# The recurrent mixer's second half as one pipeline

## Chip, cores and metric

The kernel runs on 1 core of one Trainium2 chip. The metric is the device time of one execution in microseconds.

## The reference

Two blocks of a language model run on one sequence of 256 tokens, width 1024, in float32. The second block's first mixer is the part that matters here. It projects the tokens to r, k, v and low-rank parts, and to a convolution branch. The recurrent half runs, for each of 8 heads of 64,

```python
s_kk = jnp.einsum('bhvk,bhk->bhv', state, kk_t)
state = (state * w_t[:, :, None, :] - s_kk[..., None] * (kk_t * a_t)[:, :, None, :]
         + v_t[..., None] * k_t[:, :, None, :])
y_t = jnp.einsum('bhvk,bhk->bhv', state, r_t)
```

then normalises y by head, adds a bonus `sum(r k r_k) v` and gates it. The other half is a causal convolution of 31 taps by channel (512 channels), a layer norm and a SiLU. Both halves, concatenated, go through a 1024 x 1024 output projection, an RMS norm and the next feed-forward.

## The kernel before

The five engines each run one program written by hand; semaphores order them. Weights come as units of 128 x 2048 floats by SP's queue into `wf[s]`; ScalarE copies each to a rounded high part `wh[s]` (`prep`, L614), VectorE subtracts to the low part `wl[s]` (`low`, L1070), and TensorE forms each product as three matmuls (L1790 to L1792).

The recurrence is computed in two chunks b of 128 tokens, by heads in four groups g = 2b + parity, four heads each. Rows (alpha, beta, rho, kappa) are turned to `rows_T` (L2142). Gram products of rows give, for each group, a strictly lower matrix N. Its inverse is built by merging blocks: from pairs (D and its transpose DT), in six rounds m, with Z = mask(N D), then D from DT Z, and DT from Z DT. A round has for each group four matmuls for Z ("z_mm"), a mask by VectorE (L1517, from a bank), four for D and four for DT (L2200), and copies to SBUF by ScalarE (L902). All four Z products of a round stand ahead of its D and DT products.

Before the rounds come the other Gram products: key Grams (L2179) and beta Grams (L2159), which VectorE takes from the banks with a mask (L1521 and L1517). In the rounds VectorE runs the convolution's taps (L1536) on three of the four channel tiles; the fourth tile's taps are made by ScalarE (a scaled copy, L917) and added by GpSimd (L569). GpSimd also forms products for the bonus and the gate (L547, L557, L563) and the first DT (L553). `v` is mixed with its shifted self on VectorE (L1446, L1450, L1456).

Behind the rounds: key times value (`first_w`, L2226), the solve (`solved`, L2233), the state between the chunks (L2254, L2255), the outputs (`outputs_of`, L2242, L2243), the turns of the convolution (L2262), its norm (L1611 to L1624), the head norm of y in `centred`, `spread` and `gated_y`, and the output projection (`second_exit`): block 0 is turned whole (L1837), four units are multiplied for it and, with block 1 turned in the middle, `half` is signalled. ScalarE's order at the exit is: both `take_x` (L619), `prep(4)`, `prep(5)`, the squares of block 0 (L641). The next feed-forward's loads are issued when both chunks' outputs are done.

## Time and profile before

| | |
|---|---|
| median of 3 runs | 2488.04 us (2486.35 to 2489.47) |
| profiled execution | 2487.75 us |
| its span | 2485.9 us |
| mean granted TensorE clock | 0.985 |
| TensorE, VectorE, ScalarE, GpSimd busy | 97, 59, 43, 6% |
| the stretch of the change | about 1570 to 1750 us |

PE is TensorE's matmuls, PEld its weight loads, DVE VectorE, ACT ScalarE, POOL GpSimd. A row of a timeline has its start in us, its length, engine, line, operation, tiles, shapes and count; in brackets the idle time before it and what ended it. A float32 matmul has two entries, a transpose one. `arena`, `wf`, `gains`, `y` and `hid` are memories that many names of the kernel share: `wf` holds N, D, DT and Z here. Names in the rows are those of the memory.

### The profile page before, as it was taken

Reading aid. Unit: us, or ns where it says so; the run is one execution under the profiler, and the core shown is the slowest. Engines: PE = TensorE matmul, PEld = TensorE weight load, DVE = VectorE, ACT = ScalarE, POOL = GpSimd, SP = SyncE. Lnnn points to the kernel's source line nnn. Section 1 sums busy time; section 2 is a strip of 40 time slices with the busy share of each in tenths; the row PEclk is TensorE's granted clock in tenths of the full one; section 3 lists DMA queues with packets and bytes.
Section 4 is the critical chain, followed back from the end, with each engine's and each line's share of the span. In section 5 each row is a group of like instructions: output and inputs, shape, how many; then the busy total and the mean of one; then the engine's idle time right before and its main releaser. Section 6 shows DMA issues by size and latency. Waiting matters only on the chain.

```text
span 2485.9 us, 29666 instructions
## 1 busy us (share of the span) xinstructions
PE 2399.5 (97%) x11556; PEld 1982.3 (80%) x11556; DVE 1458.1 (59%) x1569; ACT 1080.6 (43%) x1335; POOL 150.5 (6%) x178
## 2 busy tenths in 40 slices
PE   6999998999999999999999999898999999999998
PEld 5888887888888888778887887697888888777887
DVE  3545766754645667675456456984545545645544
ACT  4434445343443444544444445353444444545442
POOL 0001000000000000000000002431000000200000
PEclk9999999999999999999999999998999999999999
DMA  6666444555655564455565565203556556343552
GB/s 218 206 207 214 171 136 150 203 171 186 204 180 186 199 205 170 136 187 179 186 218 170 190 226 175 72 1 133 178 191 199 179 191 200 115 139 119 191 190 92
DMA packets 281236, 426.57 MB, mean 172 GB/s; under 512 B 11747, under 2 KB 193635, under 8 KB 281136
## 3 DMA queue, kind: packets, MB, share of 16 engines
q1 hardware_dynamic: 272768, 399.67, 48.6%
q0 software_dynamic: 7520, 25.37, 3.3%
q8 instruction: 58, 0.95, 0.2%
q10 hardware_dynamic: 864, 0.36, 0.1%
q14 instruction: 26, 0.21, 0.0%
HBM read 422.49 MB, written 1.05 MB: 170 GB/s over the span
## 4 chain that ended last, share of the span: by engine, by line
PE 82%; DVE 12%; ACT 2%; issue 2%; POOL 2%; DMA 1%; SPq 1%; DVEq 0%; POOLq 0%; ACTq 0%
PE bank L1790 24%; PE bank L1792 24%; PE bank L1791 24%; DVE wl L1070 4%; PE bank L2200 2%; PE bank L1890 1%; PE bank L1837 1%; POOL rstd L445 1%; DVE stats L1105 1%; DVE arena L1536 1%; SPq L341 1%; DVE x L1114 1%; DVE y L1172 1%; PE bank L1992 1%; DVE y L1139 1%
## 5 line engine op out<-in xcount | busy, mean ns | idle before, releaser
L1070 DVE TENSOR_TENSOR wl<-wf,wh 128x2048 fp32r<-128x2048 f32 x355 | 809.4, 2293 | 416.2 <-ACT wh L614 415.8
L1790 PE MATMUL bank<-wh,xTh 128*128 128x512 f32 x2336 | 931.5, 399 | 34.9 <-DVE xTl L1084 26.9
L1792 PE MATMUL bank<-wh,xTl 128*128 128x512 f32 x2336 | 914.4, 391 | 0.0
L1791 PE MATMUL bank<-wl,xTh 128*128 128x512 f32 x2336 | 913.6, 391 | 0.0
L614 ACT ACTIVATE wh<-wf 128x2048 fp32r<-128x2048 f32 x355 | 673.4, 1915 | 248.9 <-PE bank L1792 244.4
L1790 PEld LDWEIGHTS bank<-wh,xTh 128*128 128x128 f32 x2336 | 442.8, 190 | 128.6 <-DVE xTl L1084 29.6
L1792 PEld LDWEIGHTS bank<-wh,xTl 128*128 128x128 f32 x2336 | 442.0, 189 | 94.2
L1791 PEld LDWEIGHTS bank<-wl,xTh 128*128 128x128 f32 x2336 | 443.1, 190 | 87.6 <-issue 0.7
L1790 PE MATMUL bank<-wh,hTh 128*128 128x512 f32 x704 | 276.9, 393 | 0.1
L1792 PE MATMUL bank<-wh,hTl 128*128 128x512 f32 x704 | 274.5, 390 | 0.0
L1791 PE MATMUL bank<-wl,hTh 128*128 128x512 f32 x704 | 274.0, 389 | 0.0
L623 ACT ACTIVATE sil<-bank 128x256 f32<-128x256 f32 x176 | 60.4, 381 | 298.9 <-PE bank L1792 298.9
L1792 PEld LDWEIGHTS bank<-wh,hTl 128*128 128x128 f32 x704 | 132.1, 188 | 27.8
L1790 PEld LDWEIGHTS bank<-wh,hTh 128*128 128x128 f32 x704 | 132.2, 188 | 26.9 <-DVE wl L1070 0.3
L1791 PEld LDWEIGHTS bank<-wl,hTh 128*128 128x128 f32 x704 | 132.3, 188 | 26.5
L1089 DVE SCALAR_TENSOR_TENSOR hid<-sil,bank 128x256 f32<-128x256 f32 x176 | 68.2, 418 | 132.2 <-ACT sil L623 131.7
L445 POOL TENSOR_TENSOR rstd<-ve,mhalf 128x1 f32<-128x1 f32 x42 | 36.8, 877 | 1730.4 <-DVE ve L1109 857.8
L679 ACT ACTIVATE hTh<-bank 128x512 fp32r<-128x512 f32 x64 | 38.3, 598 | 218.7 <-PE bank L1890 218.7
L1217 DVE TENSOR_TENSOR hTl<-bank,hTh 128x512 fp32r<-128x512 f32 x64 | 44.3, 692 | 110.3 <-ACT hTh L679 110.3
L619 ACT ACTIVATE xTh<-bank 128x512 fp32r<-128x512 f32 x76 | 41.3, 596 | 104.8 <-PE bank L1837 104.4
L2200 PE MATMUL bank<-wf 128*128 128x128 f32 x544 | 64.9, 283 | 7.7 <-DVE wf L1517 7.7
L2200 PEld LDWEIGHTS bank<-wf 128*128 128x128 f32 x544 | 63.8, 198 | 8.8 <-DVE wf L1517 8.2
(317 smaller groups left out, 1554.8 us busy)
## 6 DMA issues: line engine op xcount, KB each, us to landing
wf<-in_ffn_w SPq DMA_DIRECT2D x160, 512.0 KB, 4.8
wf<-in_w_in SPq DMA_DIRECT2D x52, 1024.0 KB, 5.4
wf<-in_ffn_w SPq DMA_DIRECT2D x44, 1024.0 KB, 5.2
wf<-in_ffn_w_down SPq DMA_DIRECT2D x44, 1024.0 KB, 5.1
wf<-in_ffn_w_gate SPq DMA_DIRECT2D x80, 512.0 KB, 4.0
wf<-in_ffn_w_up SPq DMA_DIRECT2D x80, 512.0 KB, 4.9
wf<-in_w_branch SPq DMA_DIRECT2D x16, 1024.0 KB, 5.2
wf<-in_c_w_in SPq DMA_DIRECT2D x14, 1024.0 KB, 5.9
```

Source lines behind the costliest of these rows:

```text
L445: pool.tensor_tensor(dst, src, mhalf[:, 0:n], ALU.pow).then_inc(SEM[to], 1)
L614: act.activation(wh[s], wf[s], ACT.Copy).then_inc(SEM[f"hi{s}"], 1)
L619: act.activation(xTh[:, 4 * r:4 * r + 4, b * P:(b + 1) * P], bank[banks[r]][:, :].rearrange("p (k t) -> p k t", k=4), ACT.Copy).then_inc(S ...
L623: act.activation(sil[:, b, :], bank[bk][:, 0:STEP], ACT.Silu).then_inc(SEM["h_silu"], 1)
L679: act.activation(hTh[0][:, :, :], bank[6][:, :].rearrange("p (k t) -> p k t", k=2), ACT.Copy)\
L1070: dve.tensor_tensor(wl[s], wf[s], wh[s].bitcast(f32), ALU.subtract).then_inc(SEM[f"lo{s}"], 1)
L1089: return dve.scalar_tensor_tensor(hid[:, b, :], sil[:, b, :], half, bank[bk][:, STEP:2 * STEP], ALU.mult, ALU.mult)
L1217: dve.tensor_tensor(hTl[0][:, :, :], bank[6][:, :].rearrange("p (k t) -> p k t", k=2), hTh[0][:, :, :].bitcast(f32), ALU.subtract).then_in ...
L1790: pe.matmul(o, lh, rh, start=start, stop=False)
L1791: pe.matmul(o, lh, rl, start=False, stop=False)
L1792: return pe.matmul(o, ll, rh, start=False, stop=stop)
L2200: ins = pe.matmul(bank[bk][:, i * P:(i + 1) * P], left[:, i, :], right[:, i, :], start=True, stop=True)
```

## The change

The Gram products other than those of N leave their place ahead of the merges. The merges run as 24 steps i (group i % 4, round i // 4 + 1): at step i TensorE forms Z of i, then D and DT of i - 2, and from step 5 to 16 one of the twelve Gram products (`FILLS`). ScalarE copies a Gram product to SBUF and GpSimd masks it there. Taps of all four channel tiles run on VectorE, one a step, two in the odd steps from 9 on. The v mixing stands behind the first masks; its last addition is GpSimd's. The row turns of four groups are split around the last v unit. Key-times-value products and the state's kappa part stand between merges. At the exit the projection is split by its input half: convolution half first, then y's half, and each half block is turned, copied and lowered by itself. SP loads two units of the next feed-forward when the last merge product is done, two more after the outputs.

```diff
-    gram_bank = (1, 3, 0, 2)
+    start_bank, z_bank, fill_bank = (1, 3, 4, 5), (1, 3), (0, 2)
+    FILLS = [("key", u) for u in range(4)] + [("beta", g) for g in range(2)] + [("key", u) for u in range(4, 8)] + [("beta", g) for g in (2, 3)]
+    FIRST_FILL = 3
...
-        for h in range(2):
-            half_panel(w_ab, HALF, 2 + h, h)
+        half_panel(w_ab, HALF, 2, 1)
+        half_panel(w_ab, HALF, 3, 0)
         half_panel(w_ab, 0, 1, 1)
+        sp.wait_ge(SEM["dt_mm"], c.next("dt_mm", 24))
+        up(w1[0, 1], w3[0, 1], 1, 0)
         sp.wait_ge(SEM["y_mm"], c.next("y_mm", TB))
-        ffn(w1[0, 1], w3[0, 1], w2[0, 1])
+        up(w1[0, 1], w3[0, 1], 0, 4)
+        ffn(w1[0, 1], w3[0, 1], w2[0, 1], led=True, next_led=True)
...
         shift(kp, kq, "prev0_ld")
-        shift(kp, kq, "prev1_ld")
 
...
             pool.wait_ge(SEM["n_ready"], c.next("n_ready"))
-            pool.tensor_tensor(DT_t[g], N_t[g], four(pair_t), ALU.mult).then_inc(SEM["dt_ready"], 1)
+            pool.tensor_tensor(DT_t[g], N_t[g], four(pair_t), ALU.mult).then_inc(SEM["dt0_ready"], 1)
+        shift(kp, kq, "prev1_ld")
+        pool.wait_ge(SEM["v_out"], c.next("v_out"))
+        pool.wait_ge(SEM["prev1_ld"], c.next("prev1_ld", 64))
+        pool.tensor_tensor(rv_t, rv_t, kp, ALU.add).then_inc(SEM["v_in"], 1)
         pool.wait_ge(SEM["late_ld"], c.next("late_ld", 16 * 6))
-        pool.wait_ge(SEM["rk_ready"], c.next("rk_ready"))
-        product(r_t, r_t, k_new)
-        pool.tensor_tensor(r_t, r_t, both(r_k), ALU.mult).then_inc(SEM["rk_made"], 1)
-        pool.wait_ge(SEM["bonus_done"], c.next("bonus_done"))
-        for b in range(TB):
-            product(heads(r_t[:, b, :]), heads(rv_t[:, b, :]), per_head(bonus[:, 8 * b:8 * b + 8]))
-        product(r_t, r_t, both(lnx_b), ALU.add)
-        product(r_t, r_t, g_t)
-        pool.tensor_tensor(g_t, g_t, both(lnx_g), ALU.mult).then_inc(SEM["post_made"], 1)
-        pool.wait_ge(SEM["tap0"], c.next("tap0"))
-        for n in range(CONV - 1):
-            pool.wait_ge(SEM["tap_in"], c.next("tap_in"))
-            if n:
-                pool.wait_ge(SEM["tap"], c.next("tap"))
-            pool.tensor_tensor(conv_o[:, 3, :], conv_o[:, 3, :], tap_s[:, n % 4, :], ALU.add).then_inc(SEM["tap"], 1)
-        c.count("tap")
+        for f, (kind, n) in enumerate(FILLS):
+            pool.wait_ge(SEM["gram_cp"], c.next("gram_cp"))
+            if kind == "key":
+                t = k_grams[n // 2][:, 2 * (n % 2):2 * (n % 2) + 2, :, :]
+                m = gram_m.rearrange("p (a w) t -> p a w t", a=1).broadcast_to([P, 2, 2, P])
+            else:
+                t, m = b_grams[n], four(gram_m[:, 1, :])
+            pool.tensor_tensor(t, t, m, ALU.mult).then_inc(SEM["gram_made"], 1)
+            if f == 0:
+                pool.wait_ge(SEM["rk_ready"], c.next("rk_ready"))
+                product(r_t, r_t, k_new)
+            elif f == 1:
+                pool.tensor_tensor(r_t, r_t, both(r_k), ALU.mult).then_inc(SEM["rk_made"], 1)
+            elif f in (7, 8):
+                if f == 7:
+                    pool.wait_ge(SEM["bonus_done"], c.next("bonus_done"))
+                b = f - 7
+                product(heads(r_t[:, b, :]), heads(rv_t[:, b, :]), per_head(bonus[:, 8 * b:8 * b + 8]))
+            elif f == 9:
+                product(r_t, r_t, both(lnx_b), ALU.add)
+            elif f == 10:
+                product(r_t, r_t, g_t)
+            elif f == 11:
+                pool.tensor_tensor(g_t, g_t, both(lnx_g), ALU.mult).then_inc(SEM["post_made"], 1)
...
-        for g in range(4):
-            take_rows(g, ROW_A)
+        for g in (0, 2):
+            take_rows(g, ROW_A, 4 + g)
+        prep(3)
+        for g in (1, 3):
+            take_rows(g, ROW_A, 4 + g)
+        for g in range(2):
+            take_rows(g, ROW_R, 6 + g)
         prep(1)
-        for g in range(4):
-            take_rows(g, ROW_R)
-
...
-        n = 0
-        for m in range(1, 7):
-            for g in range(4):
-                if m < 6:
-                    copied(D_t, g, 4, "d_mm", "d_ready")
-                copied(DT_t, g, 6, "dt_mm", "dt_ready")
-                for _ in range(2 if g == 3 else 1):
-                    tap(n)
-                    n += 1
-        act.wait_ge(SEM["tap"], c.next("tap", CONV - 1))
-        taken(w_s, 0, 4, "w_mm", "w_ready")
-        taken(u_s, 0, 5, "u_mm", "u_ready")
-        taken(w_s, 1, 1, "w_mm", "w_ready")
-        taken(u_s, 1, 3, "u_mm", "u_ready")
+        for g in range(2, 4):
+            take_rows(g, ROW_R, 4 + g)
+        c.count("gram_mm", 4)
+        for i in range(24):
+            if i < 20:
+                copied(D_t, i, 4, "d_mm", "d_ready")
+            copied(DT_t, i, 6, "dt_mm", "dt_ready")
+            if i == FIRST_FILL:
+                act.wait_ge(SEM["v_in"], c.next("v_in"))
+            if 0 <= i - FIRST_FILL < len(FILLS):
+                take_gram(i - FIRST_FILL)
+            if i == 17:
+                taken(w_s, 0, 0, "w_mm", "w_ready")
+        act.wait_ge(SEM["rk_made"], c.next("rk_made"))
+        taken(u_s, 0, 4, "u_mm", "u_ready")
+        taken(w_s, 1, 2, "w_mm", "w_ready")
...
-        y_squares(0)
+        def out_x(b, r, bk):
+            act.wait_ge(SEM["tr"], c.next("tr"))
+            act.activation(xTh[:, 4 * r:4 * r + 4, b * P:(b + 1) * P], bank[bk][:, :].rearrange("p (k t) -> p k t", k=4), ACT.Copy)\
+               .then_inc(SEM["xt_hi"], 1)
+
         for b in range(TB):
             silu_conv(b)
+        taken(u_s, 1, 4, "u_mm", "u_ready")
+        y_squares(0)
+        out_x(0, 1, 6)
+        out_x(1, 1, 7)
         y_squares(1)
+        out_x(0, 0, 4)
+        out_x(1, 0, 5)
         c.count("gen1", 3)
         c.count("gen0", 3)
-        for b in range(TB):
-            take_x(b)
         prep(4, 2)
         prep(5, 2)
         out_of_mixer(RMS)
...
-        c.count("gen0")
-        unmixed(rv_t, mu_v, 0, 1)
...
         def tap(j):
-            if j == 0:
-                dve.tensor_scalar(conv_o[:, 3, :], gluT[:, 3, 0:T], convw[:, 3, 0:1], convw[:, 3, CONV:CONV + 1], ALU.mult, ALU.add)\
-                   .then_inc(SEM["tap0"], 1)
-            for ct in range(3):
-                dve.wait_ge(SEM["dve"], c.so_far("dve") - 2)
+            for ct in range(4):
+                dve.wait_ge(SEM["dve"], c.so_far("dve") - 3)
...
-        mixed_in(rv_t, kp, "prev1_ld").then_inc(SEM["v_in"], 1)
+        c.count("gen0")
+        unmixed(rv_t, mu_v, 0, 1)
+        dve.sem_inc(SEM["v_out"], 1)
         for g in range(4):
-            masked(D_t[g], gram_bank[g], pair_m, "turned", "d_ready")
-        dve.wait_ge(SEM["v_in"], c.next("v_in"))
+            masked(D_t[g], start_bank[g], pair_m, "turned", "d0_ready")
+        low(1)
         dve.wait_ge(SEM["cw_ready"], c.next("cw_ready"))
-        for u in range(4):
-            key_grams(u)
-        low(1)
-        for u in range(4, 8):
-            key_grams(u)
-        tap(0)
-        for g in range(4):
-            masked(b_grams[g], 4 + g, gram_m[:, 1, :], "gram_mm", "gram_ready")
-        dve.wait_ge(SEM["rk_made"], c.next("rk_made"))
-        dve.tensor_reduce(bonus, r_t.rearrange("p b (h n) -> p (b h) n", n=HD), X, ALU.add).then_inc(SEM["bonus_done"], 1)
         dve.wait_ge(SEM["lo1"], c.so_far("lo1"))
-        j = 1
-        for m in range(1, 7):
-            for g in range(4):
-                masked(Z_t[g], gram_bank[g], merge_m[m], "z_mm", "zp_ready")
-                for _ in range(2 if g % 2 and m < 5 else 1):
-                    if j < CONV:
-                        tap(j)
-                        j += 1
-        while j < CONV:
-            tap(j)
-            j += 1
+        j = 0
+        for i in range(24):
+            masked(Z_t[i % 4], z_bank[i % 2], merge_m[i // 4 + 1], "z_mm", "zp_ready")
+            if i == 8:
+                dve.wait_ge(SEM["rk_made"], c.next("rk_made"))
+                dve.tensor_reduce(bonus, r_t.rearrange("p b (h n) -> p (b h) n", n=HD), X, ALU.add).then_inc(SEM["bonus_done"], 1)
+            for _ in range(2 if i % 2 and i > 8 else 1):
+                if j < CONV:
+                    tap(j)
+                    j += 1
+        assert j == CONV
         dve.wait_ge(SEM["dve"], c.so_far("dve"))
         dve.sem_inc(SEM["conv_done"], 1)
...
-        dve.wait_ge(SEM["post_made"], c.next("post_made"))
-        centred(0)
...
+        centred(0)
+        out_x(0, 1, 6)
+        out_x(1, 1, 7)
         spread(0)
+        centred(1)
+        dve.wait_ge(SEM["post_made"], c.next("post_made"))
         gated_y(0)
-        centred(1)
         spread(1)
+        out_x(0, 0, 4)
         gated_y(1)
-        for b in range(TB):
-            take_x(b)
+        out_x(1, 0, 5)
         low(4)
         low(5)
...
         whole_unit(3, 0, outs(0))
-        whole_unit(1, 1, outs(0))
...
-        for g in range(4):
-            turn_rows(g, (alpha, beta))
+        for g in (0, 2):
+            turn_rows(g, (alpha, beta), 4 + g)
+        whole_unit(1, 1, outs(0))
+        for g in (1, 3):
+            turn_rows(g, (alpha, beta), 4 + g)
...
-        for g in range(4):
-            turn_rows(g, (rho, kappa))
-        pe.wait_ge(SEM["rows_ready"], c.next("rows_ready", 4))
-
...
+        for g in range(2, 4):
+            pe.wait_ge(SEM["rows_ready"], c.next("rows_ready"))
+            turn_rows(g, (rho, kappa), 4 + g)
+
+        def fill(f):
+            kind, n = FILLS[f]
+            if f == 0:
+                pe.wait_ge(SEM["gen0"], c.so_far("gen0"))
+            if f > 1:
+                pe.wait_ge(SEM["gram_cp"], c.next("gram_cp"))
+            o = bank[fill_bank[f % 2]]
+            if kind == "key":
+                b, par = n // 4, n // 2 % 2
+                for i in range(2):
+                    ins = pe.matmul(o[:, i * 2 * P:(i + 1) * 2 * P], row(b, par + 4 * (n % 2) + 2 * i, ROW_K),
+                                    rows_T[b][par * HD:(par + 1) * HD, 2 * (n % 2) + i, ROW_A:ROW_R + 1, :], start=True, stop=True)
+            else:
+                for q in range(4):
+                    h = 2 * q + n % 2
+                    ins = pe.matmul(o[:, q * P:(q + 1) * P], row(n // 2, h, ROW_B), row(n // 2, h, ROW_R), start=True, stop=True)
+            ins.then_inc(SEM["gram_mm"], 1)
...
-        pe.wait_ge(SEM["dt_ready"], c.next("dt_ready", 4))
-        for m in range(1, 7):
-            for g in range(4):
-                pe.wait_ge(SEM["d_ready"], c.next("d_ready"))
-                four_products(gram_bank[g], N_t[g], D_t[g], "z_mm")
-            if m == 1:
-                pe.wait_ge(SEM["gram_ready"], c.next("gram_ready", 4))
-            for g in range(4):
-                pe.wait_ge(SEM["zp_ready"], c.next("zp_ready"))
-                pe.wait_ge(SEM["dt_ready"], c.so_far("dt_ready") + max(0, g - 1))
-                if m < 6:
-                    pe.wait_ge(SEM["d_ready"], c.so_far("d_ready") + max(0, g - 1))
-                    four_products(4 + g % 2, DT_t[g], Z_t[g], "d_mm")
-                four_products(6 + g % 2, Z_t[g], DT_t[g], "dt_mm")
-            c.count("dt_ready", 4)
-
...
+        def z_products(i):
+            if i < 4:
+                pe.wait_ge(SEM["d0_ready"], c.next("d0_ready"))
+            else:
+                pe.wait_ge(SEM["d_ready"], c.so_far("d_ready") + i - 3)
+            if i > 1:
+                pe.wait_ge(SEM["zp_ready"], c.so_far("zp_ready") + i - 1)
+            four_products(z_bank[i % 2], N_t[i % 4], D_t[i % 4], "z_mm")
+
+        def merge_products(i):
+            g = i % 4
+            pe.wait_ge(SEM["zp_ready"], c.so_far("zp_ready") + i + 1)
+            if i < 4:
+                pe.wait_ge(SEM["dt0_ready"], c.next("dt0_ready"))
+            if i > 1:
+                pe.wait_ge(SEM["dt_ready"], c.so_far("dt_ready") + i - 1)
+            if i < 20:
+                if i > 1:
+                    pe.wait_ge(SEM["d_ready"], c.so_far("d_ready") + i - 1)
+                four_products(4 + g % 2, DT_t[g], Z_t[g], "d_mm")
+            four_products(6 + g % 2, Z_t[g], DT_t[g], "dt_mm")
...
+        for i in range(24):
+            z_products(i)
+            if i == 2:
+                pe.wait_ge(SEM["rows_ready"], c.next("rows_ready", 2))
+            if i > 1:
+                merge_products(i - 2)
+            if 0 <= i - 2 - FIRST_FILL < len(FILLS):
+                fill(i - 2 - FIRST_FILL)
+            if i == 18:
+                pe.wait_ge(SEM["gram_cp"], c.next("gram_cp", 2))
+                pe.wait_ge(SEM["gram_made"], c.next("gram_made", len(FILLS)))
+                pe.wait_ge(SEM["v_in"], c.next("v_in"))
+                key_values(0, 0, 0, True, True).then_inc(SEM["w_mm"], 1)
+            if i == 20:
+                key_values(1, 2, 0, True, False)
+            if i == 22:
+                pe.wait_ge(SEM["w_ready"], c.so_far("w_ready") + 1)
+                key_values(0, 0, 1, True, False)
+        pe.wait_ge(SEM["d_ready"], c.next("d_ready", 20))
+        state_of(kappa, rv_t, True, False)
+        merge_products(22)
+        pe.wait_ge(SEM["dt_ready"], c.so_far("dt_ready") + 22)
+        solved(0, 4)
+        merge_products(23)
         pe.wait_ge(SEM["u_ready"], c.next("u_ready"))
-        for h in range(RH):
-            o = bank[4][(h % 2) * HD:(h % 2 + 1) * HD, (h // 2) * HD:(h // 2 + 1) * HD]
-            pe.matmul(o, tokens(kappa, 0, h), tokens(rv_t, 0, h), start=True, stop=False)
-            ins = pe.matmul(o, tokens(beta, 0, h), tokens(u_s, 0, h), start=False, stop=True)
-        ins.then_inc(SEM["s_mm"], 1)
-        outputs_of(0, 0)
+        state_of(beta, u_s, False, True).then_inc(SEM["s_mm"], 1)
+        updates_out(0, 0)
+        pe.wait_ge(SEM["zp_ready"], c.next("zp_ready", 24))
+        key_values(1, 3, 1, True, False)
+        pe.wait_ge(SEM["state_in"], c.next("state_in"))
+        state_in(2, ROW_A, True).then_inc(SEM["w_mm"], 1)
+        state_in(3, ROW_R, False)
+        pe.wait_ge(SEM["dt_ready"], c.next("dt_ready", 24))
         pe.wait_ge(SEM["conv_done"], c.next("conv_done"))
-        pe.wait_ge(SEM["tap"], c.next("tap", CONV - 1))
...
+        for b in range(TB):
+            pe.wait_ge(SEM["yb_ready"], c.next("yb_ready"))
+            turn_half(y_conv[:, b, :], 6 + b)
+        pe.wait_ge(SEM["ya_ready"], c.next("ya_ready"))
+        turn_half(y_rwkv[:, 0, :], 4)
+        x_in()
+        part_unit(1, 1, 0, 0, True, False)
+        part_unit(2, 1, 0, 1, True, False)
+        x_in()
+        x_in()
+        part_unit(0, 0, 0, 0, False, True)
+        part_unit(3, 0, 0, 1, False, True).then_inc(SEM["half"], 1)
+        part_unit(1, 1, 1, 2, True, False)
+        pe.wait_ge(SEM["yc_ready"], c.next("yc_ready", TB))
+        pe.wait_ge(SEM["ya_ready"], c.next("ya_ready"))
+        turn_half(y_rwkv[:, 1, :], 5)
+        part_unit(2, 1, 1, 3, True, False)
+        x_in()
+        part_unit(0, 0, 1, 2, False, True)
+        turn(0, y, "x_ready")
+        part_unit(3, 0, 1, 3, False, True)
+
```

## Rows read from the trace of the kernel before

**Rows 1.** The page, part 1: busy time and share of the span

```profile
PE 2399.5 (97%) x11556; PEld 1982.3 (80%) x11556; DVE 1458.1 (59%) x1569; ACT 1080.6 (43%) x1335; POOL 150.5 (6%) x178
```

**Rows 2.** The chain that ended last, 1560 to 1760: start, us, what

```profile
1609.07 6.89 DVE arena L1536 x6
```

**Rows 3.** Windows: busy us and count by engine, granted clock, DMA share, GB/s

```profile
1603.00:1616.00 13.00, 6.40 (x55) 6.02 (x54) 13.00 (x13) 3.18 (x6) 10.96 (x7) 1.00 0.00 1
1616.60:1673.50 56.90, 56.42 (x483) 55.91 (x483) 50.25 (x104) 32.68 (x65) 19.30 (x25) 0.97 0.00 1
1673.50:1711.00 37.50, 25.84 (x192) 24.83 (x191) 15.73 (x30) 8.33 (x15) 7.57 (x9) 0.74 0.22 68
```

**Rows 4.** Timeline of VectorE: start, us, line, operation, count, idle before

```profile
1579.67 1.29 DVE L1517 TENSOR_TENSOR wf<-bank,gains 128x512 f32<-128x512 f32 x2
...
1585.60 2.29 DVE L1456 TENSOR_TENSOR arena<-arena 128x1024 f32<-128x1024 f32 x1
...
1603.30 0.68 DVE L1517 TENSOR_TENSOR wf<-bank,gains 128x512 f32<-128x512 f32 x1
...
1605.89 2.57 DVE L1536 SCALAR_TENSOR_TENSOR arena<-y,arena 128x256 f32<-128x256 f32 x1
1608.39 0.68 DVE L1517 TENSOR_TENSOR wf<-bank,gains 128x512 f32<-128x512 f32 x1
1608.99 4.45 DVE L1536 SCALAR_TENSOR_TENSOR arena<-y,arena 128x256 f32<-128x256 f32 x2
...
1618.26 2.45 DVE L1536 SCALAR_TENSOR_TENSOR arena<-y,arena 128x256 f32<-128x256 f32 x6
...
1671.96 0.64 DVE L1581 MEMSET y<- 64x256 f32 x2
```

**Rows 5.** Timeline of GpSimd, 1581 to 1622

```profile
1581.71 2.81 POOL L553 TENSOR_TENSOR wf<-wf,gains 128x512 f32<-128x512 f32 x2 [2.09 <-DVE wf L1543]
...
1603.46 2.23 POOL L547 TENSOR_TENSOR arena<-arena,gains 128x512 f32<-128x512 f32 x2 [9.72 <-DVE gains L1565]
1605.77 2.41 POOL L547 TENSOR_TENSOR arena<-arena,sil 128x1024 f32<-128x1024 f32 x1
...
1621.26 0.72 POOL L569 TENSOR_TENSOR arena<-arena 128x256 f32<-128x256 f32 x1 [6.38 <-ACT arena L917]
```

**Rows 6.** Timeline of TensorE, 1576 to 1675

```profile
1576.11 1.91 PE L2142 MATMUL bank<-ident,arena 128*128 128x128 f32 x16
1577.97 1.16 PE L2159 MATMUL bank<-rows_T 64*128 64x128 f32 x16
...
1586.32 2.96 PE L2179 MATMUL bank<-rows_T 64*128 64x256 f32 x16
...
1616.61 54.34 PE L2200 MATMUL bank<-wf 128*128 128x128 f32 x464 [5.44 <-DVE wf L1517]
...
1673.30 1.90 PE L2226 MATMUL bank<-arena 128*128 128x64 f32 x16
```

**Rows 7.** Timelines of all engines in the tail and the exit, 1691 to 1735

```profile
1691.27 0.70 DVE L1611 BATCH_NORM_STATS2 stats<-bank 128x6 f32<-128x512 f32 x1
...
1695.09 1.42 DVE L1624 SCALAR_TENSOR_TENSOR arena<-arena,rstd 128x512 f32<-128x512 f32 x2
...
1711.01 0.76 PE L1790 MATMUL bank<-wh,xTh 128*128 128x512 f32 x1 [7.11 <-DVE xTl L1084]
...
1720.17 3.72 ACT L614 ACTIVATE wh<-arena 128x2048 fp32r<-128x2048 f32 x2
1722.12 4.50 DVE L1070 TENSOR_TENSOR wl<-arena,wh 128x2048 fp32r<-128x2048 f32 x2 [1.00 <-ACT wh L614]
1725.10 0.60 ACT L641 ACTIVATE y<-bank 128x512 f32<-128x512 f32 x1 [1.20 <-PE bank L1792]
1727.88 1.92 ACT L614 ACTIVATE wh<-wf 128x2048 fp32r<-128x2048 f32 x1 [1.51 <-PE bank L1792]
1733.69 1.09 PE L1837 MATMUL bank<-ident,y 128*128 128x128 f32 x8 [0.47 <-DVE y L1128]
```

173 lines of the change are left out of this document (75 added, 98 removed).

## The prediction

> **What bounds the kernel now.** I read the page first: TensorE is busy 97% of the span [rows 1]. The change touches only the recurrent mixer's second half, about 1570 to 1750 us, so I read that stretch by windows [rows 3], where three kinds of time show. From 1603 to 1616 VectorE is busy all 13.0 us and TensorE 6.4. From 1616.6 to 1673.5 TensorE is busy 56.4 of 56.9. From 1673.5 to 1711 nobody is full and the granted clock averages 0.74. The chain of work that ended last says the same: it runs through VectorE taps up to 1616 (6.89 us for six of them [rows 2]) and then through merge products that follow each other without a wait [rows 6].
>
> **One VectorE tap and one GpSimd instruction.** Six taps in a row take 2.45 us [rows 4]; with 0.47 us for the last that is a pitch of 0.396. The tap that starts at 1605.89, just behind a GpSimd product of 2.41 us, takes 2.57 [rows 4, 5]. A mask that reads a bank starts inside the next GpSimd product, takes its usual 0.68 and hands over 0.60 later, at 1608.99 [rows 4]. So a tap, with both its tiles in SBUF, waits for GpSimd, and a mask does not. The rate comes from 1603.90 to 1615.88: 11.98 us hold nine taps (3.56) and one mask (0.60), so 7.8 us are waiting, while GpSimd was busy about 10.5 us (10.96 in the window less 0.44 before [rows 3, 5]). That is 0.74 us of VectorE per microsecond of GpSimd.
>
> The Trainium skill ("SBUF — State Buffer", the section on the two separate sides) has a rule that speaks against this change: VectorE with two SBUF inputs and GpSimd take turns on one port pair as an exclusive lock, and the loser waits for the whole instruction. By that rule the price would be 1.0 per microsecond, and the sum below some 8 us longer; the row's 2.57 beside 2.41 agrees with it, and the average 0.74 only says how often something else fills the wait.
>
> **The front, to the first merge mask.** The first Gram mask is at 1579.67 now [rows 4]. The change puts two groups of row turns (0.5 each, four take 1.91) ahead of the last v unit, which ends 1576.1 now; one group and a Gram set (1.2) follow [rows 6]: last turn 1577.5, copy 0.6, Gram set 1578.3 to 1579.5. The mask starts where it did. Masks and identities go on to 1585.6 as now [rows 4]. Then the v mixing (2.6), four masks (2.4) and the unit's low part (2.29) come: first merge mask at 1593.0, against 1603.30 [rows 4]. A gain of 10.3 us at this point, all of it from Gram masks and a bonus reduction moved behind it.
>
> **The pipeline on TensorE.** 58 products in 54.34 us are 0.937 each [rows 6]. From the first mask's end 66 of the 68 remain: 61.8. Filling: a key pair of half-array matmuls takes 0.75 to 0.86 (four pairs in 2.96 [rows 6] where pairs of both halves overlap; alone 4 x 0.216), a beta set 0.9; twelve come to 10.6. Three sets of key times value at 1.9 [rows 6], the kappa part 0.9 and the first solve 1.9 now stand before the last merge: 8.5. Sum 80.9, end 1674.6 if nothing waits. The merges end now just before the key times value set at 1673.30 [rows 6]. So on TensorE alone the pipeline gives nothing but later work done early (about 10 us of it).
>
> **The pipeline on VectorE.** 24 masks at 0.60 are 14.4; 31 taps of four instructions, 124 at 0.396, are 49.1 (34 more instructions than now); the reduction 1.2. Sum 64.7. The Gram masks are no longer there, and the taps that GpSimd and ScalarE did are. On GpSimd: v addition 2.4; twelve Gram products at 1.26 (a masked 128x512 product is between 1.04 and 1.40, [rows 5]), 15.1; two 128x1024 products 4.8, two halves 2.2, three more 7.2. Sum 31.7, all beside taps; today 30 additions of 0.73 lie there and 14 us of products, part of these beside bank masks. At 0.74 VectorE waits 23.5. Together 88.2: VectorE ends its taps at **1681**, against 1671.96 now, where the state's memset starts [rows 4]. Bounds: rate 0 leaves TensorE's 1674.6 as the limit (taps end near 1672); rate 1.0 gives 1689. I take 0.74, because the products at 1603 to 1615 are the same instructions beside the same taps. A check by parts: steps 0 to 8 have slack on VectorE (2.18 a step against 3.7 on TensorE) and hide some waits; steps 9 to 17 have none: 27.6 clean plus 0.74 x 21 of GpSimd is 43, against 34 on TensorE. In these steps TensorE waits for masks.
>
> **The tail to the first exit unit.** Around the last mask TensorE still owes the products of sets 21 to 23, kappa part and first solve (6.5), a copy (0.8), then beta part, outputs, key times value, state products and conv transposes (7.4): transposes end about 1692.7. The conv normalisation takes 5.2 (1691.27 to 1696.51, [rows 7]). ScalarE has the copy of the second solve queued behind both SiLUs: it lands near 1699, though the solve ended near 1695. Outputs 1.8, turns 0.9, copy and two low parts 1.9; VectorE's second centring is queued behind these low parts. Spread, centring and gating are six instructions 512 wide at 0.7 and two small ones (4.6 with their waits for each other), the turn 0.5: 1708.7. About 2 us more for the lower clock, which this tail has now too (0.74), gives 1710.7. The first exit unit is at 1711.01 now, after a wait of 7.11 [rows 7]. So the overlap of conv half and y half is real, and the 9 us late pipeline eats it.
>
> **The exit.** Four units from the first to the end of `half` take 13.9 now with a turn in between (1711.01 to 1725.0), without it 13.1: 1723.8. ScalarE squares at once today (1725.10), because both copies of the next feed-forward's units were done while TensorE worked (1720.17, 3.72) [rows 7]. After the change the turn of y's second block stands behind part unit (1,1,1), and ScalarE's order is turn copy, two unit copies, squares: 1723.8 + 2.7 + 0.5 + 0.8 + 3.7 = 1731.5. VectorE's second low part ends at 1733.9, against 1726.6 now [rows 7]. From there to the turn of the new x is 7.1 as now [rows 7]: **1741.0 against 1733.69**, +7.3. TensorE ran out of work near 1733 and waits 8 us; behind the 7.11 us wait at 1711 now, ten matmuls have a pitch of 0.43 (the first takes 0.76, [rows 7]) where the later ones have 0.23, and the same again costs 2.0.
>
> **Units loaded early** I cost at nothing. The copy at 1727.88 waits for TensorE (1.51), not for a load, and those at 1720.17 wait for the turn [rows 7]. If that cover were gone, a late load could cost at most what the copies that wait for it take, 3.7 us; an earlier one gives back nothing.
>
> **Sum.** +7.3 + 2.0 = +9.3 on the profiled execution's 2487.75 (span 2485.9 and 1.85 around it; median of the runs 2488.04, so no correction): **2497 us**. Within 0.2% (5 us) counts as no change.
>
> **Rivals.**
> 1. *TensorE bounds the pipeline*; GpSimd's instructions fall where VectorE waits anyway. For it: slack of 1.5 us in each early step. Against: from step 9 every second step has eight tap instructions. Taps end 1672, first exit unit 1702, turn of x 1732.5, with the clock's 2 us: 2488.5, no change. It ends on the faster side, at 2482, where TensorE in the tail then keeps the upper clock of 2.4 GHz (this tail's clock of 0.74 [rows 3] loses about 6). It decides where VectorE's exposed waiting is under 15 us instead of 23.5 (rate 0.47); above 19 us the time leaves the 5 us that count as no change.
> 2. *The clock falls inside the pipeline.* Today 5.4 us of waiting before 1616.61 is followed by a stretch at the lower of the two levels (1.2 GHz); in steps 13 to 16 TensorE has about 4 us of work in 10. Each 3 products there cost 2.3 more: +5 to +8, 2502 to 2505.
> 3. *The loads or the v shift are late.* The v addition waits for a transfer issued behind four GpSimd products; if the first Gram copy waits for it, +3: 2500.
>
> **Chances.** Forecast 0.54; rival 1 0.28 (half of it below 2483); rival 2 0.12; rival 3 0.06. The likeliest case's own range, from GpSimd products at 1.04 or 1.40 and the rate 0.6 to 0.85, is 2492.5 to 2502. For 8 in 10: 2487 to 2504. Faster takes rival 1's lower half (0.15); the same its upper half and the lowest tenth of the other cases (0.23); slower is the rest, 0.62.
>
> **What would show it.** First mask of the merges near 1593; VectorE full from there to about 1681 with tap instructions well above 0.47 wherever GpSimd runs; TensorE waiting for VectorE masks in the middle third; a wait of ScalarE for the last turn, and squares near 1731; TensorE idle for about 8 us before the turn of x. I am wrong if taps keep 0.47 beside GpSimd products, if TensorE's products run in one piece, or if the squares start with `half`.

## The result and the profile after

The changed kernel takes 2498.94 us (2497.18 to 2500.59), the kernel before 2488.04 us: the ratio is 1.0040, with a 95% interval of 1.0028 to 1.0052. It is slower by 10.9 us (medians of five runs each); the forecast was 2497 us, 9 above before. The profiled execution took 2500.59 us, its span is 2498.8.

The page, busy time and share of the span, after (before [rows 1]):

```profile
PE 2405.2 (96%) x11556; PEld 1984.3 (79%) x11556; DVE 1469.6 (59%) x1586; ACT 1077.5 (43%) x1317; POOL 146.6 (6%) x161
```

The page can't tell where 11 us went. The stretches do: windows of the changed kernel (busy us and count by engine, granted clock, DMA share, GB/s), from the first merge mask to the middle of the merges, to the taps' end, to the first exit unit, to the end of the exit's units, and to the turned new x (before [rows 3]).

```profile
1595.40:1649.00 53.60, 51.66 (x392) 46.65 (x392) 53.30 (x83) 23.30 (x39) 25.11 (x16) 1.00 0.00 1
1649.00:1683.00 34.00, 29.83 (x257) 29.27 (x258) 33.98 (x67) 9.45 (x16) 7.71 (x4) 0.95 0.00 1
1683.00:1712.00 29.00, 17.02 (x137) 16.22 (x136) 12.91 (x27) 7.76 (x12) 2.77 (x3) 0.75 0.46 145
1712.00:1730.00 18.00, 17.53 (x70) 14.51 (x71) 3.95 (x7) 0.82 (x2) 2.82 (x3) 0.84 0.47 177
1730.00:1746.00 16.00, 7.43 (x33) 6.08 (x33) 11.76 (x12) 9.01 (x12) 1.13 (x2) 0.76 0.00 0
```

In both halves of the pipeline VectorE (third pair) is full, and TensorE is nearly full in the first and loses 4 of 34 us in the second. Behind the pipeline TensorE has 17 of 29 us of work, and in the last window 7.4 of 16, at 0.76 of its clock.

Timeline of VectorE, after (before [rows 4]):

```profile
1581.97 1.29 DVE L1547 TENSOR_TENSOR wf<-bank,gains 128x512 f32<-128x512 f32 x2 [2.49 <-PE bank L2181]
...
1595.38 0.69 DVE L1547 TENSOR_TENSOR wf<-bank,gains 128x512 f32<-128x512 f32 x1
...
1605.68 1.67 DVE L1560 SCALAR_TENSOR_TENSOR arena<-y,arena 128x256 f32<-128x256 f32 x4
...
1610.44 7.06 DVE L1560 SCALAR_TENSOR_TENSOR arena<-y,arena 128x256 f32<-128x256 f32 x4
...
1641.05 8.17 DVE L1560 SCALAR_TENSOR_TENSOR arena<-y,arena 128x256 f32<-128x256 f32 x8
...
1663.47 3.25 DVE L1560 SCALAR_TENSOR_TENSOR arena<-y,arena 128x256 f32<-128x256 f32 x8
...
1683.20 0.64 DVE L1593 MEMSET y<- 64x256 f32 x2 [0.22 <-DVE arena L1560]
```

Four taps take 1.67 us alone and 7.06 beside GpSimd, eight take 3.25 or 8.17. What stood beside them, in GpSimd's timeline (before [rows 5]):

```profile
1609.54 1.28 POOL L570 TENSOR_TENSOR arena<-arena,gains 128x512 f32<-128x512 f32 x1 [12.04 <-ACT arena L923]
1610.77 2.55 POOL L551 TENSOR_TENSOR arena<-arena 128x1024 f32<-128x1024 f32 x1
1613.41 1.31 POOL L570 TENSOR_TENSOR arena<-arena,gains 128x512 f32<-128x512 f32 x1
1614.68 2.53 POOL L575 TENSOR_TENSOR arena<-arena,row 128x1024 f32<-128x1024 f32 x1
...
1646.40 2.53 POOL L551 TENSOR_TENSOR arena<-arena,sil 128x1024 f32<-128x1024 f32 x1
```

And TensorE, which waits for the masks behind such groups, and then in the tail (before [rows 6, 7]):

```profile
1649.96 4.39 PE L2217 MATMUL bank<-wf 128*128 128x128 f32 x24 [1.85 <-DVE wf L1547]
...
1661.52 2.92 PE L2217 MATMUL bank<-wf 128*128 128x128 f32 x24 [3.21 <-DVE wf L1547]
...
1693.04 1.04 PE L2309 MATMUL bank<-ident,arena 128*128 128x128 f32 x8
...
1700.90 3.68 PE L2263 MATMUL bank<-arena 128*128 128x64 f32 x16 [5.09 <-ACT arena L932]
...
1712.47 1.12 PE L2317 MATMUL bank<-ident,arena 128*128 128x128 f32 x4 [6.19 <-DVE arena L1620]
1713.24 0.78 PE L1810 MATMUL bank<-wh,xTh 128*128 128x512 f32 x1
...
1743.78 1.97 PE L1857 MATMUL bank<-ident,y 128*128 128x128 f32 x8 [8.57 <-DVE y L1160]
```

The last row is the exit's end: TensorE had nothing to do for 8.57 us and turned the new x at the lower clock (1.97 us for eight, 1.09 before). Why x was late is in ScalarE's timeline (before [rows 7]):

```profile
1699.07 1.29 ACT L961 ACTIVATE arena<-arena 128x512 f32<-128x512 f32 x2 [4.82 <-DVE arena L1640]
1700.27 0.58 ACT L932 ACTIVATE arena<-bank 128x512 f32<-128x512 f32 x1
...
1729.78 0.60 ACT L969 ACTIVATE xTh<-bank 128x512 fp32r<-128x512 f32 x1 [15.56 <-PE bank L2317]
1730.27 3.71 ACT L630 ACTIVATE wh<-arena 128x2048 fp32r<-128x2048 f32 x2
1733.89 0.58 ACT L657 ACTIVATE y<-bank 128x512 f32<-128x512 f32 x1
```

The copy of the second solve (1700.27) stands behind two SiLUs that waited 4.82 us for the normalisation. Later ScalarE waited 15.56 us for one turn, did two unit copies behind it, and only then the squares that everything else waited for.

### The profile page after: what moved, and what is told of

Same layout as the page of the kernel before. It is cut to its first block, busy times and chain, and to the rows that moved or that the text cites. A ratio compares the mean times of both kernels' runs of the same rounds, so it can differ in the third digit from the quotient of the medians.

```text
span 2498.8 us, 29644 instructions
## 1 busy us (share of the span) xinstructions
PE 2405.2 (96%) x11556; PEld 1984.3 (79%) x11556; DVE 1469.6 (59%) x1586; ACT 1077.5 (43%) x1317; POOL 146.6 (6%) x161
## 4 chain that ended last, share of the span: by engine, by line
PE 81%; DVE 12%; ACT 2%; issue 2%; POOL 1%; DMA 1%; SPq 1%; DVEq 0%; POOLq 0%; ACTq 0%
PE bank L1810 24%; PE bank L1812 24%; PE bank L1811 24%; DVE wl L1102 4%; DVE arena L1560 2%; PE bank L1910 1%; PE bank L1857 1%; PE bank L2217 1%; POOL rstd L450 1%; DVE stats L1137 1%; SPq L342 1%; DVE wf L1547 1%; DVE x L1146 1%; DVE y L1204 1%; PE bank L2012 1%
## 5 line engine op out<-in xcount | busy, mean ns | idle before, releaser
L1811 PEld LDWEIGHTS bank<-wl,hTh 128*128 128x128 f32 x704 | 132.3, 188 | 26.5
```

The costliest lines, as they stand in the source:

```text
L1811: pe.matmul(o, lh, rl, start=False, stop=False)
```

## The experiments

Every trace of a variant is read the same way, in four distances; the first Gram mask's start is the origin, since the changed kernel and its variants are alike up to it (the kernel before has its row turns and last v unit in another order) and it moves from 1577.28 to 1582.72 between traces. The memset stands right behind VectorE's last tap, so the first distance gives the taps' end. Each is worked out from rows of the timelines (starts of the mask, the memset, the first exit unit, the turn of the new x; the last column is the span less that turn). The ratio is to the kernel before on the same chip; an interval is 0.0009 to 0.0014 to each side, so 2 to 3.5 us, and two variants whose ratios are closer than that are told apart by their traces at best.

| kernel | mask to memset | to first exit unit | to turn of x | turn of x to end | median us | ratio |
|---|---|---|---|---|---|---|
| before | 92.3 | 131.3 | 154.0 | 752.2 | 2488.04 | 1 |
| changed | 101.2 | 131.3 | 161.8 | 755.0 | 2498.94 | 1.0040 |
| forecast | 101.3 | 131.0 | 161.3 | 754.2 | 2497 | 1.0036 |
| y's turn early | 101.3 | 131.3 | 158.5 | 754.8 | 2495.76 | 1.0029 |
| old exit | 101.2 | 132.3 | 154.8 | 751.2 | 2490.21 | 0.9998 |
| solve's copy first | 101.8 | 126.7 | 157.4 | 755.1 | 2493.74 | 1.0017 |
| Gram masks on VectorE | 103.6 | 133.5 | 163.0 | 753.9 | 2499.75 | 1.0045 |
| three tiles | 96.8 | 127.1 | 157.7 | 754.7 | 2493.2 | 1.0013 |
| late products | 94.3 | 124.5 | 155.0 | 755.1 | 2491.53 | 1.0008 |
| three orders | 102.7 | 129.0 | 150.6 | 752.0 | 2485.98 | 0.9984 |
| old exit, copy first | 103.4 | 133.2 | 156.7 | 752.6 | 2489.65 | 0.9995 |
| conv units first | 100.6 | 122.6 | 148.4 | 751.4 | 2484.27 | 0.9983 |
| the same, late products | 94.3 | 114.4 | 140.8 | 751.8 | 2473.6 | 0.9942 |
| the same, centring first | 94.3 | 114.1 | 140.4 | 751.8 | 2473.87 | 0.9941 |
| late loads | 101.2 | 131.3 | 161.8 | 757.0 | 2497.53 | 1.0037 |

**Theory and rivals.** My theory had two places of loss: GpSimd's products hold up VectorE's taps in the pipeline, and the turn of y's second block, in ScalarE's queue ahead of the squares, delays the exit. The rivals: TensorE bounds the pipeline whatever VectorE does; the clock falls inside it.

**y's turn early.**

```diff
         part_unit(1, 1, 0, 0, True, False)
         part_unit(2, 1, 0, 1, True, False)
+        pe.wait_ge(SEM["ya_ready"], c.next("ya_ready"))
+        turn_half(y_rwkv[:, 1, :], 5)
...
-        pe.wait_ge(SEM["ya_ready"], c.next("ya_ready"))
-        turn_half(y_rwkv[:, 1, :], 5)
         part_unit(2, 1, 1, 3, True, False)
```

> The changed kernel, but TensorE turns y's second block before the part units (0,0,0) and (3,0,0) instead of behind (1,1,1); nothing else moves. Theory (the exit's order makes the squares late, and the idle time behind them costs clock): the copy of that turn is at about 1722 instead of 1729.8, both unit copies are done by 1726, the squares start with half at about 1727 instead of 1733.9, the new x is turned at about 1736 instead of 1743.8, TensorE's wait before it shrinks from 8.57 to about 1 us and the last part unit runs at the upper clock. Time 9 to 10 us less than the changed kernel, 2489 to 2490. Rival (the squares wait for half anyway and only the pipeline is late): the same time as the changed kernel, 2499.

That came out far short. The squares came 6.8 us earlier (145.2 behind the origin against 151.9), the turn of x only 3.3, and the ratio fell by 0.0011, 2.7 us instead of 9 to 10; the two ratios' intervals overlap, so the gain is shown by the trace and not by the times. Where the rest stayed is in ScalarE's timeline of this run:

```profile
1722.43 0.60 ACT L657 ACTIVATE y<-bank 128x512 f32<-128x512 f32 x1 [1.27 <-PE bank L1812]
...
1730.65 1.91 ACT L630 ACTIVATE wh<-wf 128x2048 fp32r<-128x2048 f32 x1 [6.95 <-PE bank L1812]
1732.47 1.04 ACT L662 ACTIVATE y<-x 128x1024 f32<-128x1024 f32 x1
```

The third unit's copy waits 6.95 us for TensorE to give its buffer back, and the squares of the new x, ready since 1727.57, stand behind it. One queued wait was taken away and the next was exposed.

**Old exit.** The pipeline as changed, TensorE's, VectorE's and ScalarE's exit and SP's order of the projection's units as before.

```diff
-        half_panel(w_ab, HALF, 2, 1)
-        half_panel(w_ab, HALF, 3, 0)
+        for h in range(2):
+            half_panel(w_ab, HALF, 2 + h, h)
...
-        out_x(0, 1, 6)
-        out_x(1, 1, 7)
...
+        for b in range(TB):
+            take_x(b)
```

> The changed kernel's pipeline with the exit of the kernel before (both blocks turned whole, four units for block 0, take_x on both engines, unit order by column). Theory: the first exit unit comes about 5 us later than in the changed kernel (1718.5, behind the second gating and two low parts), half is then near 1732, but the squares start with it and TensorE does not idle before the new x's turn: turn at about 1741, upper clock behind it, time 2494 to 2496, 3 to 5 us less than the changed kernel. Rival (splitting the projection by input is itself worth its 7 us and the pipeline alone is the loss): 2503 or more.

It gave back 0.0042, 10.5 us, more than expected: 7.0 us to the turn of x and 3.9 behind it, where TensorE waits 0.48 us instead of 8.57 and keeps its clock; the rows up to the next feed-forward's first turn of `hid` place 2.3 us of the 3.9 (11.9 us there against 14.1). So with the old exit the new pipeline is worth nothing either way (0.9998). That doesn't put the whole loss in the exit: the late products below take back 8 of the same 11 us with the exit left as changed.

**Solve's copy first.**

```diff
+        taken(u_s, 1, 4, "u_mm", "u_ready")
         for b in range(TB):
             silu_conv(b)
-        taken(u_s, 1, 4, "u_mm", "u_ready")
```

> The changed kernel, but ScalarE copies the second solve before the two SiLUs instead of behind them. Theory (in-order ScalarE holds TensorE for 5.09 us at 1700.9): the outputs of chunk 1 start near 1696.5, the turns of the convolution half follow the SiLUs at about 1700.4 instead of 1703.5, everything behind is 3 to 4 us earlier: 2495 to 2496. Rival (the convolution norm sets the tail anyway): under 1 us, 2498 to 2499.

The first exit unit came 4.6 us earlier, the turn of x 4.4. The ratio fell by 0.0023 (5.7 us), a little more than the 3 to 4 us expected. With the *old* exit the same edit did nothing that can be told:

> The pipeline of the changed kernel with the exit of the kernel before (measured alone: 2490.2), and the copy of the second solve before both SiLUs. Theory: TensorE waits 5.08 us there for that copy, and gets 4 of them back: 2485 to 2487. Rival (the conv turns and VectorE's normalisation end last there, the wait is hidden): 2489 to 2491.

0.9995 against 0.9998. TensorE's wait for the copy went from 5.08 to 0.69 us there, too, but its next wait, for VectorE's gating of y, grew from 3.85 to 8.30: in the old order nothing of the exit starts before both halves of block 0 are turned. The pipeline of that trace is also 2.2 us longer: one more wait of 0.69 us, one of 3.95 instead of 3.17, and the lower clock took 2.3 us (three merge products, 24 entries, in 5.25 us instead of 2.92) where it took 1.5 in the old exit's trace. Its turn of x is only 1.9 later, so at most 0.3 us of gain can lie behind the pipeline. The expected 3 to 5 us are not there.

**Gram masks on VectorE.** All twelve by VectorE straight from the bank, steps 6 to 17; ScalarE's copies and GpSimd's masks fall away.

```diff
             masked(Z_t[i % 4], z_bank[i % 2], merge_m[i // 4 + 1], "z_mm", "zp_ready")
+            if 0 <= i - 6 < len(FILLS):
+                mask_gram(i - 6)
```

> The changed kernel, but the twelve Gram products are masked by VectorE from the bank, one a step behind the merge mask, instead of being copied by ScalarE and masked by GpSimd in SBUF. Theory (VectorE is the pipeline's bound and waits 0.74 us for each microsecond of GpSimd): VectorE's own work grows by 12 x 0.60 = 7.2, its waiting shrinks by 0.74 x 15.8 = 11.7; the taps end about 4 us earlier (1679 instead of 1683.0) and the time is 2494 to 2496. Rival (TensorE bounds the pipeline): taps end within 1 us of where they did, time 2498 to 2500. Second rival (VectorE is the bound but GpSimd costs it nothing): 7 us later, 2506.

No gain: taps end 2.4 us later. The rival's number came out, but for another reason. Without the waits for Gram copies between them, GpSimd's first two 128x1024 products moved to the pipeline's start. Timelines of GpSimd, VectorE and TensorE in this run:

```profile
1596.19 2.39 POOL L551 TENSOR_TENSOR arena<-arena 128x1024 f32<-128x1024 f32 x1
1598.66 2.34 POOL L568 TENSOR_TENSOR arena<-arena,row 128x1024 f32<-128x1024 f32 x1
```

```profile
1594.71 6.76 DVE L1535 TENSOR_SCALAR arena<-y,arena 128x256 f32<-128x256 f32 x4
```

```profile
1602.22 10.75 PE L2210 MATMUL bank<-wf 128*128 128x128 f32 x72 [4.36 <-DVE wf L1525]
```

The first four taps took 6.76 us, TensorE waited 4.36 for the mask behind them, and its next nine products ran partly at the lower clock (10.75 against 8.28 in the changed kernel). That is 6.6 us lost where the changed kernel loses 0.2, against some 4 won later. So the experiment moved a cost besides removing one, and doesn't tell the two theories apart.

**Late products** does. Nothing is left out; only five products of GpSimd move behind the taps.

```diff
+        pool.wait_ge(SEM["bonus_done"], c.next("bonus_done"))
+        pool.wait_ge(SEM["conv_done"], c.next("conv_done"))
+        for b in range(TB):
+            product(heads(r_t[:, b, :]), heads(rv_t[:, b, :]), per_head(bonus[:, 8 * b:8 * b + 8]))
...
```

> Changed kernel, its work whole: GpSimd's last five products (10 us, at 1638 to 1660 beside taps) wait until VectorE has ended its taps, and lie then in time where VectorE waits for TensorE. Theory (port waits of VectorE make TensorE's two waits for masks of 1.85 and 3.21 us, and the lower clock after the first of them 1.4 more): these go, taps end 5 to 6.5 us earlier, 2493 to 2495. Rival (the twelve Gram masks of GpSimd are enough to hold VectorE up, or the tail waits for the late products): 2498 to 2502.

The ratio fell by 0.0032 (8 us, 1.5 beyond the theory's range), the taps end 6.9 us earlier. The waits of 1.85 and 3.21 us are gone, and the three products (24 entries) behind the first are back from 4.39 to 2.9: together 6.5. VectorE and GpSimd in this run:

```profile
1631.52 1.32 POOL L570 TENSOR_TENSOR arena<-arena,gains 128x512 f32<-128x512 f32 x1 [2.67 <-ACT arena L919]
...
1635.44 1.27 POOL L570 TENSOR_TENSOR arena<-arena,gains 128x512 f32<-128x512 f32 x1 [2.61 <-ACT arena L919]
...
1674.66 2.17 POOL L551 TENSOR_TENSOR arena<-arena,gains 128x512 f32<-128x512 f32 x2 [22.17 <-DVEq L1587]
```

```profile
1630.84 4.26 DVE L1556 SCALAR_TENSOR_TENSOR arena<-y,arena 128x256 f32<-128x256 f32 x8
...
1635.62 2.56 DVE L1556 SCALAR_TENSOR_TENSOR arena<-y,arena 128x256 f32<-128x256 f32 x4
```

One Gram mask of 1.27 to 1.32 us costs a group of taps 0.9 to 1.0 us (2.56 instead of 1.66, 4.26 instead of 3.25), and TensorE's step of 3.9 us hides that. The five products beside the others it could not hide.

**Three tiles.** It leaves out 30 of the fourth channel tile's 31 taps.

```diff
-            for ct in range(4):
-                dve.wait_ge(SEM["dve"], c.so_far("dve") - 3)
+            for ct in range(4 if j == 0 else 3):
+                dve.wait_ge(SEM["dve"], c.so_far("dve") - (3 if j == 0 else 2))
```

> Leaves out part of the computation: the fourth channel tile gets only its first convolution tap (30 of 124 tap instructions fewer, 11.9 us of VectorE and the waits for GpSimd in them). Theory (TensorE's own pipeline of about 83 us lies 6.7 us under what it takes now, so only so much is to be had): 2492 to 2494, TensorE without waits for masks inside the pipeline. Rival (VectorE alone sets the pipeline's length): 12 us or more off, 2486 to 2488. Other rival (the exit sets the end): 2499.

Taps end 4.4 us earlier, the ratio fell by 0.0027: the theory's time. By the times that can't be told from late products (0.0032); by the traces thirty taps fewer bring the taps' end 4.4 us forward and five GpSimd products moved bring it 6.9, at 124 taps. TensorE is not free of waits, as the theory had it: it still waits 2.68 us for one mask, at 1654.81, behind the products of GpSimd that are still there. So VectorE's count of taps doesn't set the pipeline: TensorE's own work does, plus the places where GpSimd's products come thick.

**Three orders**, that is the early turn, the solve's copy first, and the squares of x ahead of the third unit's copy in ScalarE's queue (only this third edit is shown):

```diff
-        out_of_mixer(RMS)
+        square_sum(0)
+        new_square_sum(0)
+        prep(0, 2)
+        take_x(0)
```

> Changed kernel with three orders altered, its work whole: TensorE turns y's second block before the units that it doesn't need (as in the run of that alone), ScalarE copies the second solve before both SiLUs, and ScalarE takes the squares of the new x before the copy of the third unit, behind which they waited 6.95 us in the run with the early turn (squares at 1732.47, while x was ready at 1727.57). Theory (three instructions each queued behind a wait that they don't need, prices add): 2500 on this chip less 4.2 and 6.2 as measured alone, less 5 us for the squares and 3 to 4 us for the lower clock behind the idle time before the turn of x that then is gone: 2481 to 2483, that turn at about 1 us instead of 1.97. Rival (the exit has one chain of dependent steps that takes its time, whatever the order): gains don't add, 2488 to 2491.

0.9984, 14 us under the changed kernel, 3 to 5 short of the sum expected. The pipeline of this trace was 1.5 us longer, by waits for masks (6.5 us instead of 5.1). The turn of x took 1.09 us behind a wait of 0.38, and the time behind it was 752.0 instead of 755.0. TensorE's timeline shows the next wrong order:

```profile
1699.11 1.97 PE L2320 MATMUL bank<-ident,arena 128*128 128x128 f32 x8 [1.26 <-ACT arena L961]
1707.89 1.11 PE L2320 MATMUL bank<-ident,arena 128*128 128x128 f32 x4 [6.81 <-DVE arena L1623]
1708.66 0.78 PE L1813 MATMUL bank<-wh,xTh 128*128 128x512 f32 x1
```

The conv half is turned at 1701 and lowered at 1703, and its units wait for y's turn, which they don't need.

**Conv units first.** TensorE's order on top of that:

```diff
-        pe.wait_ge(SEM["ya_ready"], c.next("ya_ready"))
-        turn_half(y_rwkv[:, 0, :], 4)
         x_in()
         part_unit(1, 1, 0, 0, True, False)
         part_unit(2, 1, 0, 1, True, False)
         pe.wait_ge(SEM["ya_ready"], c.next("ya_ready"))
-        turn_half(y_rwkv[:, 1, :], 5)
+        turn_half(y_rwkv[:, 0, :], 4)
         x_in()
+        part_unit(1, 1, 1, 2, True, False)
+        pe.wait_ge(SEM["ya_ready"], c.next("ya_ready"))
+        turn_half(y_rwkv[:, 1, :], 5)
...
-        turn(0, y, "x_ready")
         part_unit(3, 0, 1, 3, False, True)
+        turn(0, y, "x_ready")
```

> The kernel with three orders altered (2486.0), and TensorE's exit ordered anew, its work whole: the two conv units of the first token block stand ahead of the turn of y's first block (they waited behind it until 1708.59 in that trace, while their data were ready at 1703.06), the turn of y's second block comes one unit later, and the last unit stands ahead of the turn of the new x. Theory (TensorE's fixed order, not the work, sets the exit): the units start near 1703.5 and end before the turn of x; squares some 2 us earlier, and 2.75 us of the last unit no longer behind that turn: 2481 to 2483. Rival (the chain over ScalarE's copies, VectorE's low parts and the two normalisations takes what it takes): 2485 to 2487.

The first unit came 6.3 us earlier, the turn of x 2.2, and the ratio is the same (0.9983); the time lies between the theory's and the rival's. Of these gains 2.1 us are not the edit's: this trace's taps end 2.1 us earlier (100.6 against 102.7) with the same pipeline. Counted from the memset the first unit comes 4.3 us earlier and the turn of x 0.1. From 1687 to 1695, ahead of the first unit, TensorE ran at the lower clock (0.61 granted), its matmuls following each other:

```profile
1685.92 0.69 PE L2273 MATMUL bank<-arena 128*64 128x64 f32 x16 [1.18 <-ACT arena L932]
1686.53 2.41 PE L2266 MATMUL bank<-arena 128*128 128x64 f32 x16
1688.73 3.62 PE L2247 MATMUL bank<-arena 128*128 128x64 f32 x16
1692.15 3.27 PE L2253 MATMUL bank<-y,rows_T 128*128 128x128 f32 x16
```

The last three take 9.3 us; in the changed kernel the same three take 2.00, 1.95 and 2.00, so 3.3 us are the clock's. Between the first unit and the turn of x stand now the last unit (2.7 us), a turn (0.4) and a wait of 0.7; the last unit had filled TensorE's wait behind that turn, which grew from 0.75 to 1.71 us.

**The same with late products.** Both edits in one kernel.

> As the run with the conv units first, and GpSimd's last five products behind VectorE's taps, which alone gave 7.3 us on the changed kernel. Theory (the two are in places of their own, one in the pipeline, one in the exit, and add): 6.5 to 7.3 us under that run, 2474 to 2476. Rival (with the pipeline shorter, the loads of the next feed-forward's units or of the projection's come too late, and the exit waits for them): 2479 to 2482.

2473.6 us, ratio 0.9942 (0.9928 to 0.9955): 14.5 us faster than the kernel before, about 24 than the changed one by the ratios, and with the next run the lowest of all. Against the run with the conv units first the ratio fell by 10 us, more than the theory's 6.5 to 7.3; the distances give 7.2 (7.6 at the turn of x, 0.4 back behind it), and the rest is within the intervals. The turn of x is 21 us nearer the origin than in the changed kernel, behind a wait of 0.40 us. From the memset it takes 46.5 us, 1.4 less than in three orders, so the new order of the units is worth that much in a trace in which the clock cost 1 us there instead of 3.3. The rival's late loads cost nothing that shows.

**The same, centring first.**

```diff
+        y_squares(0)
         taken(u_s, 1, 4, "u_mm", "u_ready")
         for b in range(TB):
             silu_conv(b)
-        y_squares(0)
...
+        centred(0)
         dve.wait_ge(SEM["convT"], c.next("convT", TB))
         for b in range(TB):
             conv_stats(b)
+        spread(0)
...
-        centred(0)
         out_x(0, 1, 6)
         out_x(1, 1, 7)
-        spread(0)
```

> As the run with the conv units first and the late products, and VectorE centres the first block of y before the convolution's normalisation, where it waits 5.56 us for TensorE, with ScalarE's square of it ahead of the second solve's copy. Theory (VectorE's 17 us of instructions between the conv transposes and the last gating set when y's second block can be turned): 1 to 2 us under that run. Rival (that block is covered by the conv units now): the same within 0.5 us, or 1 us more, because the conv half comes later.

No difference (0.9941): the rival. Centring y earlier brings the first exit unit 0.3 us, and the turn of y's first half (122.0 to 121.7 behind the origin) no more. That the conv units cover it is argued and not shown.

**Late loads.**

```diff
-        sp.wait_ge(SEM["dt_mm"], c.next("dt_mm", 24))
-        up(w1[0, 1], w3[0, 1], 1, 0)
         sp.wait_ge(SEM["y_mm"], c.next("y_mm", TB))
-        up(w1[0, 1], w3[0, 1], 0, 4)
-        ffn(w1[0, 1], w3[0, 1], w2[0, 1], led=True, next_led=True)
+        ffn(w1[0, 1], w3[0, 1], w2[0, 1])
```

> Changed kernel, only the loads of the next feed-forward's units put back behind y_mm, as in the kernel before. My prediction costs the early loads at nothing: 2498 to 2500. Rival (they bring the unit copies forward): 2502 to 2504.

1.0037 against 1.0040, with the distances unchanged to the turn of x. The trace is 2.0 us longer behind it, which the runs' medians don't confirm. Early loads are worth nothing here.

## Why the prediction was right, point by point

- **Front.** The first merge mask was forecast 13.3 us behind the first Gram mask; it is at 13.4. Everything in the trace stands 2.3 us later already ahead of the stretch. I had no term for that; traces of kernels that are the same up to this point differ by up to 5.4 us, so it can't be read as a cost of the change.
- **One tap, one GpSimd instruction, and the rate.** Taps' end at 101.3 was forecast, 101.2 came out, and steps 9 to 17 took 42.8 us (mask at 1623.87 to mask at 1666.64) for the 43 forecast. The rate itself was 0.68, not 0.74: of 87.6 us from the first merge mask VectorE's own work is 64.7 by the prediction's sum and 0.3 are waits for TensorE, which leaves 22.6 for 33 us of GpSimd (31.7 in the sum). Two small errors cancel; that the forecast came within 0.1 us is luck. By the Trainium skill ("SBUF — State Buffer", the section on the two separate sides) the loser of the port pair waits for the whole instruction. That would be 33 us here, 10 more than was paid. Part of the difference can be masks, which keep their 0.68 us beside GpSimd; how much, no run shows. As a price by the microsecond, 0.7 is what this case shows.
- **The pipeline on TensorE.** 80.9 us without a wait was forecast; from the first mask to the last merge product it is 89.6, of which 5.3 are waits for masks and 1.5 the lower clock in three products: 82.8. The term that was too small is the twelve Gram sets: 1.06 to 1.09 us each, 12.8 in all, for 10.6. Some 6.8 us of the 89.6 are VectorE's and GpSimd's doing, all of which late products gave back. From 1597 to 1648 TensorE has no wait of over 0.3 us, as forecast for the early steps; both real waits lie in the steps with eight taps.
- **Rival 1** (TensorE bounds it) fell, since moving GpSimd's work alone gave 8 us, but its limit is real: it put the taps' end 92.3 us behind the origin, and late products bring it to 94.3.
- **Rival 2** happened on a small scale: 1.5 us for the three products behind the wait of 1.85 us (2.3 in the prediction, several times over), 1.4 to 1.5 in five other traces, and in two nothing there but 1.5 and 2.3 behind a later wait of 3.95. So from there on it fell once in each of these eight traces, behind a wait for a mask, and where it falls differs between executions of one pipeline.
- **The tail and exit.** First exit unit forecast at 131.0, found at 131.3; turn of x at 161.3, found at 161.8. The wait of ScalarE for the last turn (15.56 us), the squares behind two unit copies and TensorE's idle 8.57 us are the steps as put. What I called real, the overlap of conv half and y half, was not: the conv units stood behind y's turn. The forecast came out even so, because its sum had placed the first exit unit behind the gating, as the code has it.
- **The clock behind the wait**: 2.0 forecast, 2.8 measured (755.0 less 752.2). The rows place 2.3 of it: eight matmuls at the lower level (1.5) and the turn of x itself (0.8), which my sum had left out. The other 0.5 isn't placed, and this column ranges from 753.9 to 757.0 behind the same idle time of about 8.55 us.
- **Units loaded early** at nothing: confirmed.

The sum was +9.3 and the medians differ by 10.9. The two traces differ by 12.9: 2.3 ahead of the stretch, 7.8 in it for 7.3, and 2.8 for 2.0 behind it.

## What to carry to other kernels

When a phase is cut finer so that parts may overlap, write down for every engine what stands in front of each instruction that others wait for: here a turn, a copy and a pair of squares, each queued behind a wait that it didn't need, cost 14 us, and taking one away can expose the next: the early turn alone gave 2.7 us of the 9 expected, and the solve's copy, which gave 5.7 with the new exit, gave nothing with the old one. Put a helper engine's large two-input work where the engine that it locks out waits anyway; moving 10 us of it gave 8 us, at least as much as taking away 30 of 124 taps (6.7). An overlap is only there if the engine's own program order lets the ready part start; what it then gives depends on what stands behind it, here 1.4 us in one trace and 0.1 in the other.
